# A fused decode step on one NeuronCore: one pass over all tokens, or four token chunks with the next chunk's projections between the expert picks

## What is computed

```python
proj = rms_norm(x, g_mix) @ w_in            # xa (512), xb, gb, ga, gb_pre (1024 each)
ya = s5_branch(xa, ...)                     # grouped complex linear recurrence over time, then a gelu and a gate (w_glu)
yb = rglru_branch(xb, gb, ...)              # conv of 4, two gates, h[t] = a[t] h[t-1] + b[t], per channel
merged = sigmoid(ga_pre) * (ya @ w_a) + sigmoid(gb_pre) * (yb @ w_b)
x = x + merged @ w_out
x = x + peer(rms_norm(x, g_ffn))            # below
gate = sigmoid(rms_norm(x, g_ple) @ w_ple_gate)
x = x + (p @ w_ple) * gate                  # per-layer embedding, then the final norm

def peer(t):                                # t: 128 tokens at a time, 8 heads
    s = (t @ w_q) . sub_keys                # two scores of 128 keys for each head
    sv, si = top_k(s, 16)                   # best 16 keys of each half
    cand = sv[0][:, None] + sv[1][None, :]  # 256 sums, best 16: the picks
    idx = take(si[0] * 128 + si[1], top_k(cand, 16))
    coef = softmax(top) * gelu(sum(u_tab[idx] * t))
    return sum(coef * v_tab[idx])           # u and v rows: 4 KB each, 8 heads x 16 picks per token
```

## Time and profile before

| | us |
|---|---|
| median of 3 runs (4274.88 to 4293.29) | 4286.01 |
| the profiled execution | 4287.05 |
| its span, first to last instruction | 4285.3 |
| busy in it: PE / DVE / POOL / ACT | 3612.8 / 2364.4 / 1513.4 / 1304.4 |
| data moved, mean rate | 1207.39 MB, 282 GB/s |

### The profile page before, as it was taken

One profiled execution on the slowest core, in us unless ns is written; L12 is line 12 of the kernel. 1 busy time (PEld: TensorE's weight loads), 2 busy tenths in 40 slices (PEclk: granted clock), 3 DMA queues, 4 the chain that ended last, 5 costly groups with the idle time before them and its releaser, 6 DMA issues.

```text
span 4285.3 us, 40997 instructions
## 1 busy us (share of the span) xinstructions
PE 3612.8 (84%) x9599; PEld 1758.8 (41%) x9599; DVE 2364.4 (55%) x5593; ACT 1304.4 (30%) x3634; POOL 1513.4 (35%) x1507
## 2 busy tenths in 40 slices
PE   7999999999999677877877877887887787787787
PEld 5655666664566233333323333332333333333322
DVE  7266220001366766666666666666665666666675
ACT  2233310001100233433433333343343333343343
POOL 0365100000000354444445444444445444444542
PEclk8999699999999899999999999999999898999998
DMA  1111011101201899999999999999999999999995
GB/s 72 36 33 35 23 70 34 39 22 54 88 30 40 366 417 414 396 416 407 377 417 412 389 407 410 401 396 415 399 400 413 393 400 414 417 391 417 415 369 226
DMA packets 182142, 1207.39 MB, mean 282 GB/s; under 512 B 26128, under 2 KB 29840, under 8 KB 41936
## 3 DMA queue, kind: packets, MB, share of 16 engines
q0 software_dynamic: 156672, 1140.92, 65.3%
q1 hardware_dynamic: 25312, 64.93, 4.6%
HBM read 1199.31 MB, written 4.88 MB: 281 GB/s over the span
## 4 chain that ended last, share of the span: by engine, by line
PE 47%; DMA 18%; DVE 15%; issue 10%; POOL 5%; ACT 3%; SPq 0%; POOLq 0%; DVEq 0%; ACTq 0%
DMA ring<-in_uv,idxu 18%; PE psC L720 17%; PE psA L457 7%; PE psB L457 6%; PE psA L671 5%; POOL ring L430 5%; PE psB L741 3%; DVE ring L1427 3%; PE psC L659 2%; PE psB L659 1%; DVE hot L1390 1%; DVE hot L1392 1%; DVE pick L1394 1%; PE psC L485 1%; DVE dn L1250 1%
## 5 line engine op out<-in xcount | busy, mean ns | idle before, releaser
L720 PE MATMUL psC<-ring,dg 128*128 128x512 f32 (+1 forms) x4352 | 2107.3, 637 | 582.7 <-ACT dg L973 582.2
L430 POOL DMA_INDIRECT ring<-in_uv,idxu x1088 | 1325.3, 1218 | 1797.9 <-PE psC L720 1294.1
L1427 DVE CUSTOM_DVE_ANT_0 ring<-ring,xn2c 128x1024 f32<-128x1024 f32 x1088 | 1312.1, 1225 | 813.4 <-DMA ring<-in_uv,idxu 801.5
L720 PEld LDWEIGHTS psC<-ring,dg 128*128 128x128 f32 (+1 forms) x4352 | 846.7, 201 | 1826.3 <-issue 1825.6
L963 ACT ACTIVATE act<-dot 128x2 f32<-128x2 f32 x544 | 110.7, 203 | 1680.9 <-DVE dot L1427 1679.9
L973 ACT ACTIVATE dg<-ident,coef 128x128 f32<-128x128 f32 x1024 | 360.3, 394 | 38.8 <-PE psC L720 37.3
L967 ACT ACTIVATE coef<-act,gw 128x1 f32<-128x1 f32 x1088 | 261.1, 287 | 17.8
L671 PE MATMUL psA<-xn2T,w_q 128*128 128x384 f32 (+1 forms) x768 | 238.3, 471 | 3.9 <-ACT xn2T L942 3.9
L421 POOL MEMSET sv<- 128x32 f32 x1 | 0.1, 124 | 625.0 <-DVE x L1306 625.0
L671 PEld LDWEIGHTS psA<-xn2T,w_q 128*128 128x128 f32 x768 | 144.9, 190 | 91.8 <-issue 5.8
L741 PE MATMUL psB<-wgate,xn3T 128*128 128x512 f32 (+1 forms) x288 | 135.1, 595 | 0.0
(11 more groups left out here) (306 smaller groups left out, 2993.4 us busy)
## 6 DMA issues: line engine op xcount, KB each, us to landing
ring<-in_uv,idxu POOLq DMA_INDIRECT x1088, 11.4
w_q<-in_w_q SPq DMA_DIRECT2D x16, 512.0 KB, 3.5
w_xb<-in_w_xb SPq DMA_DIRECT2D x8, 512.0 KB, 3.5
w_gb<-in_w_gb SPq DMA_DIRECT2D x8, 512.0 KB, 3.5
w_ga<-in_w_ga SPq DMA_DIRECT2D x8, 512.0 KB, 3.4
w_gp<-in_w_gp SPq DMA_DIRECT2D x8, 512.0 KB, 3.5
w_yb<-in_w_yb SPq DMA_DIRECT2D x8, 512.0 KB, 3.5
wout<-in_w_out SPq DMA_DIRECT2D x1, 4096.0 KB, 12.2
```

The costliest lines, as they stand in the source:

```text
L430: pool.indirect_dma_start(out=ring[:, k % RING, :], out_offset=None, in_=a["uv"], in_offset=bass.IndirectOffsetOnAxis(ap=idxu[:, s, k:k + ...
L720: ins = nc.tensor.matmul(acc[0:rows, 512 * half:512 * (half + 1)], dg[:, k % 4, 0:rows], ring[:, k % RING, D + 512 * half:D + 512 * (half ...
L1427: ins = v.tensor_tensor_reduce(ring[:, r, 0:D], ring[:, r, 0:D], xn2c[:], 1.0, 0.0, ALU.mult, ALU.add, dot[:, k:k + 1])
```

## The change

The tokens are cut into four chunks of two tiles (256 tokens; the last chunk has the 64 sample tokens too, 320). Chunk 0's front part runs alone. After that, the front part of chunk c+1 is a second stream of work which every engine's program carries between its instructions for the picks of chunk c. Between the picks of chunk 3 stand the embeddings of all nine tiles. The recurrences carry their state in `nlru`, `nconv` and `carry`. All code is written out, no hardware loops are left. The order is fixed when the program is built: on PE a credit of `rate` us is added after each pick and spent on front matmuls (a matmul of n columns is costed at the larger of 0.21 and 0.00168 n us), so that the front of the next chunk fits in all but the last 32 and another 62 (`GAPS`) of the chunk's picks; `till(pick)` holds the stream back until a pick number where a result of another engine is awaited. ScalarE, VectorE and GpSimd place their parts by the pick numbers that PE's part left in `mark` (`Side.upto`). Every weight of the front part streams once per chunk through five 512 KB buffers (`wr`), 47 MB a chunk with tokens and keys. The S5 blocks are reordered through DRAM: `xaT` to `su`, and from there in eight transfers to `uT`; `yg` in eight transfers to `sy`, from there to `yaT`. The S5 matrices are put in DRAM once and read back per chunk. The eight `ring` slots, the four `dg`, the gathers and the two matmuls of a pick stay as they were; `choose` is cut in three (`choose_best`, `choose_places`, `choose_rows`) behind the dots of the first, second and third pair of a head.

```diff
-CHUNKS = [(0, 384), (384, 384), (768, 320)]
+KEEP = 6
+WRING = 5
+SPANS = [(0, 2), (2, 2), (4, 2), (6, 2)]
+def us(cols):
+    return max(0.21, 0.00168 * cols)
+def front_us(k):
+    wide = 60 * KD + 12 * 4 + 2 * KD
+    return (wide * us(k.n) + 160 * us(k.nbt) + len(k.tiles) * (16 * us(P) + 16 * us(512) + 16 * us(P)))
+GAPS = 62
...
+        def product(c, name, j, bank, moving):
+            w = weights(c, name, j).rearrange("p (k n) -> p k n", n=P)
+            n, kn = PARTS[c].n, moving.shape[1]
+            for k in range(kn):
+                ins = nc.tensor.matmul(psF[:, bank, 0:n], w[:, k, :], moving[:, k, 0:n], start=(k == 0), stop=(k == kn - 1))
...
+                if k % 2:
+                    yield 2 * us(n)
...
+        def s5_states(c):
+            yield from till(mark[c, "xa", 3] + 14)
+            pe.wait_ge(g.ut_in, 16 * STEP * (c + 1))
...
+            yield from till(mark[c, "cx", 3] + 12)
+            pe.wait_ge(g.ya_in, 16 * (c + 1))
+            for m in range(4):
+                yield from product(c, "glu", m, 2 + m, yaT)
...
-        with pe.Fori(1, NT - 1) as t:
-            tile(t, P, True)
+        for cost in front(0, EARLY):
+            pass
+        for p in PARTS:
+            if p.c + 1 < NCH:
+                side = front(p.c + 1, lo)
+                rate = front_us(PARTS[p.c + 1]) / (hi - lo - 2 * TOPK - GAPS)
+            else:
+                side = embeddings()
+                rate = 1.4
...
+                for G in range(first_slot(o), first_slot(o + 1)):
+                    pe.wait_ge(g.diag_ok, G + 1)
+                    for half in range(2):
+                        ins = nc.tensor.matmul(acc[0:rows, 512 * half:512 * (half + 1)], dg[:, G % DIAGS, 0:rows],
+                                               ring[:, G % RING, D + 512 * half:D + 512 * (half + 1)],
+                                               start=False, stop=(G == first_slot(o + 1) - 1))
+                    ins.then_inc(g.slot_free, 1)
+                    now[0] = G
+                    credit = min(credit + rate, 4.0)
+                    while credit > 0:
+                        cost = next(side, None)
...
+        def s5_input(c):
+            sp.wait_ge(g.xa_ok, 4 * (c + 1))
+            sp.dma_start(a["su"].rearrange("(f p) x -> p f x", p=P)[:, :, 0:k.n], xaT[:, :, 0:k.n]).then_inc(g.su_out, 16)
+            sp.wait_ge(g.su_out, 16 * (c + 1))
+            for j in range(STEP):
+                sp.dma_start(uT[GC * j:GC * (j + 1), :, 0:k.nbt],
+                             a["su"].rearrange("(g c) x -> c g x", c=GC)[:, :, j * k.nbt:(j + 1) * k.nbt]).then_inc(g.ut_in, 16)
```

More of the change, by code:

```diff
@@ L579, in _, with till, weights @@
-        with pe.Fori(0, KD - 1) as h:
-            lru_inputs(h)
-            lru_gates(h)
-        pe.wait_ge(g.chain_ok, 2)
-        for b in range(8):
-            if b >= 2:
-                pe.wait_ge(g.y2_out, 2 * b - 2)
-            for ps, n, s0 in ((psA, NB, 0), (psB, SB, NB + 1)):
+        now = [EARLY]
+        free = [True]
+        def till(at):
+            while not free[0] and now[0] < at:
+                yield None
+        def weights(c, name, j):
+            i = AT[c, name, j]
+            pe.wait_ge(w_in[i % WRING], 16 * (i // WRING + 1))
+            return wr[:, i % WRING, :]
@@ L710, in _ @@
-        scores(HEADS - 1, 0)
-        scores(HEADS - 1, 1, psA)
-        nc.tensor.transpose(psC[:, 0, 0:P], ident[:], ident[:]).then_inc(g.slot_free, over_keys)
-        def experts(first, rows, picks, last=False, between={}):
-            for k in range(picks):
-                pe.wait_ge(g.diag_ok, first + (k + 1))
-                alone(pe)
-                for half in range(2):
-                    ins = nc.tensor.matmul(acc[0:rows, 512 * half:512 * (half + 1)], dg[:, k % 4, 0:rows],
-                                           ring[:, k % RING, D + 512 * half:D + 512 * (half + 1)],
-                                           start=False, stop=(last and k == picks - 1))
-                ins.then_inc(g.slot_free, 1)
-                for step in between.get(k, ()):
-                    step()
@@ L797, in _ @@
+        free[0] = True
+        now[0] = SLOTS
+        for cost in side:
+            pass
     @block.scalar
@@ L1038, in _ @@
+        side.rest()
     @block.vector
@@ L1332, in best_keys @@
[L1332 removed]
+            own(v.max(top[:, 0:8], cand[:]))
             alone(ve)
[L1334 to L1336 removed]
+            own(v.match_replace(crep[:], top[:, 0:8], cand[:], BELOW))
             alone(ve)
[L1338 to L1342 removed]
@@ L1357, in kept @@
[L1357 to L1382 removed]
+            own(v.max(top[:, 8:16], crep[:]))
@@ new lines, in embeddings @@
+            yield from before(0)
+            yield from turned(0)
+            for o in range(NT):
+                ahead = o + 1 < PARTS[-1].first
+                if ahead:
+                    yield from before(o + 1)
+                yield from gated(o)
+                if ahead:
+                    yield from turned(o + 1)
+                yield from finish(o)
+                if not ahead and o + 1 < NT:
+                    yield from before(o + 1)
+                    yield from turned(o + 1)
```

2308 lines of the change are left out of this document (1183 added, 1125 removed).

## The result

The changed kernel takes 3959.2 us (median of 4 runs, 3946.8 to 3967.3) against 4286.0 us before (4 runs beside them): a ratio of 0.924, 95% interval 0.921 to 0.927. The profiled execution took 3967.32 us with a span of 3965.5. Faster was forecast, but at 4110 us: the time lies inside the range, close to its low end of 3950, and outside the 4020 to 4200 that the forecast gave to its own case. It is the time of rival A, the sum without stalls (3963).

The account below looks back on a forecast made before the run. The front was taken as bound by PE, the picks by DMA; overlapped, PE bounds the interleaved picks. The sum without stalls, 3963 us, plus 147 of waits made 4110, range 3950 to 4340, against 4286 before.

Parts of the forecast that it names:

- its own case: Whole kernel: the sum plus stalls in the interleaved fronts, 4110 us, between 4020 and 4200; chance 0.43.
- rival A: Whole kernel: no stalls, leads of four diagonals and eight slots cover every wait, 3963 us or 3930; chance 0.25 for below 4020.
- the sum without stalls: First pick at 460, chunks of 831, 831, 909 and 897, tail 35: 3963 us.
- that sum: Chunks 0 and 1: 162 picks at PE's 3.61 us and 94 at DMA's 2.62, 831 us each.
- 49 us a chunk: Waits in each of three interleaved fronts: RG-LRU 24, two reorderings 20, norm and transposes 5; 147 us in all.
- 20 of it for transfers that were covered: Two S5 reorderings through DRAM per chunk: PE waits between nothing and 34 us each, taken as 10.
- the RG-LRU's: Interleaved RG-LRU heads: PE, VectorE and ScalarE at similar load wait for each other, 3 us a head, 24 a chunk.

Follow-up runs that it names:

- experiment 5: Five kernels, each the changed kernel with one planner number edited (GAPS 32, 78, 84 in chunk 2; matmul price 0.09; last-chunk rate 0.9): 3980.6, 4009.4, 3956.8, 3988.9, 3962.7 us.

## What to carry to other kernels

Where one stream is bound by DMA and another by TensorE and they are interleaved, sum each engine's work per step and take the larger, as a first figure: that sum came within 6 us in 835, in part by two errors against each other, and it did not foretell what a change of pace would do (experiment 5). Add a stall for a wait whose cover you have counted and found short; here 49 us a chunk was guessed, 20 of it for transfers that were covered, and 9 to 18 came. Look for stalls under the row of the instruction that stands behind the late result too: the RG-LRU's were under the picks' diagonals. Then look at what is queued behind a transfer on the issuing queue rather than at its bytes, and when tuning the pace of an interleave, read the in-order waits after each step, since the pace can be wrong in both directions.

## What the runs showed of the hardware

- Sixteen transfers of 64 KB in 128-byte pieces, issued together on SP's queue under the gathers, held it for 30.93, 19.41 and 37.99 us in three chunks, while the median from issue to landing was 2.2 us. Single issues had a median of 505 ns and a longest of 18.97 us. Eight in the changed kernel took 15.42 us at 745.56. The cost falls on whatever is issued next there.
- A DMA share of 0.98 at 378 GB/s does not say that DMA is the bound: where PE was busy all the time, lowering the share from 0.98 to 0.72 changed the number of picks by one in 46. Bare gathers moved 420 GB/s at a share of 1.01; whether the mix of gathers and weights could reach that is not shown.
- S5's matmuls of 32 and 40 columns took 0.31 us each with weights of 128 rows and 128 columns (L461), 0.16 with 64 rows (L471) and 0.09 with 64 columns (L439), between picks.
